# Eight convolution taps of each layer move from VectorE to GpSimd, and two output weight blocks are split by ScalarE

## The chip, the cores and the metric

The kernel runs on one core of a Trainium2 chip. The metric is the device time of one execution in microseconds, as the median of several runs. Weights and inputs start in device memory (HBM), and the result is written there.

## What is computed

Two layers of a hybrid block (layers 0 and 1) over 16 learned meta rows and 512 input rows, and then one second block over the 512 rows. All data are float32. The part that the change touches is the convolution branch of each layer, a causal depthwise convolution of width 31 over 512 channels, and the output projection that adds it to the attention branch:

```python
def conformer_conv_branch(a, g, z, w_dw, b_dw, ln_g, ln_b):
    u = a * jax.nn.sigmoid(g)
    u = lax.conv_general_dilated(u, w_dw[:, None, :], window_strides=(1,),
        padding=[(CONV_WIDTH - 1, 0)], ..., feature_group_count=D_CONV) + b_dw
    u = jax.nn.silu(layer_norm(u, ln_g, ln_b))
    return u * jax.nn.silu(z)
...
    y_attn = dsa_sparse_attention(q, k, v, qi, ki, wi, topk) * jax.nn.silu(za)
    y = jnp.einsum('ble,ed->bld', jnp.concatenate([y_conv, y_attn], axis=-1), w_out[l])
    h = layer_norm(DEEPNORM_ALPHA * h + y, post_ln_g[l], post_ln_b[l])
```

Beside it each layer projects its input to q, k, v, to gates za and zc and to an indexer (qi, ki, wi). The indexer's scores select 132 keys for each query, and the attention runs over these alone.

## The kernel before

**Products in two parts.** TensorE runs in float32r, a shorter float32. To keep the accuracy each operand is split into a high part, the rounded value (`x_hi`, `w_hi`), and a low part, what is left (`x_lo`, `w_lo`), and each product is three passes: hi*hi, hi*lo, lo*hi. The weights stream in as 69 blocks of 128x2048 (`weight_stream`, L106) through a ring of four buffers. SyncE loads a block into `w_raw` once TensorE has done the last product of the block four places earlier (L614). ScalarE copies it rounded into `w_hi` and its negative into `w_lo` (`split_hi`, L693). GpSimd then starts a DMA that adds the block from HBM to the negated copy (`split_lo`, L1158, its DMA is L1162), and TensorE waits for that DMA (L1352). For the blocks in `LO_BY_POOL` (L274) ScalarE makes only `w_hi`, and GpSimd subtracts it from `w_raw` itself in two halves (`subtract_hi`, L1150, L1155). Such a subtraction and such a DMA sit in GpSimd's program at a fixed place. `SPLIT_AT` (L196) says behind which use of a product each block is split: block k2 behind the first product of q, v0 (the first half of v's weights) behind the third, v1 behind the first of k, the first za block behind the third of k.

**Order of a layer.** Each engine has its program in a fixed order. In layer l TensorE runs the products for a and g, the indexer, its scores, then q and k (four channel tiles each, some 6 us a tile), the values of the meta rows (`meta_values`, L1419, which uses v0 and then v1), v, the first gates, and then 40 attention items in layer 0 and 32 in layer 1 (an item is a tile of up to 128 queries and one of 8 heads). Items go in pairs. In each pair TensorE turns the probabilities (L1484, L1490), ScalarE copies them (`probs_t`, L842), TensorE multiplies by v (L1509, L1512) and makes logits for a later pair (L1448), VectorE adds the mask and scales (`masked_logits`, L2021), ScalarE takes the exponentials (L828), and VectorE normalises (L2028, L2030).

**What is woven into the items.** `attention_extras` (L297) hands each engine a list of extra operations for each item. TensorE's fillers are the gates (`GATE_ITEMS`, L226, items 0 to 14) and the output products `wo` (`OUTPUT_AT`, L252: item, half of the columns, row tile, PSUM buffer). The convolution's layer norm runs at items 8 to 20 (`CONV_AT`, L246): turned forward by TensorE (L1533), statistics and two scalings by VectorE (`conv_normed`, L1990, L1997), turned back (L1542), tanh by ScalarE, y by VectorE (L2065, L2069), its high part by ScalarE (L853) and its low part by GpSimd (L1182). `SPLITS_AT` (L278) says at which two items ScalarE splits the halves of a block; GpSimd's part follows in the second of them.

**The taps.** `TAPS` (L283) is the order of the 4 x 31 taps of a layer, four channel tiles c with 31 taps each, all done by VectorE: `conv_acc` becomes u shifted times a weight per channel plus `conv_acc` (`conv`, L1873). Tap 0 is a `tensor_scalar` with the bias (L1884), every other is a `scalar_tensor_tensor` (L1887) that waits for the tap before it of the same channel tile. VectorE does 62 taps before the top-k, then the 17 rounds of the top-k (`topk`, L1923: maxima L1937 and replacements L1946 over score rows of up to 528), 28 taps behind them (up to `TAPS_MASKED`), 7 after the first masked scores (`TAPS_AHEAD`), and 27 in the first eight items (`TAPS_BY_ITEM`). While VectorE is in the top-k, GpSimd waits for a result of its second round (`first_tile_cut`, L1235), and then turns q and k (`rope`, L1186: three `tensor_tensor` of 128x528 for each of 8 channel tiles), with the DMA issues of `next_blocks` between them.

Of the kernel before, what the change touches and what calls it, by code (L numbers as in the profile page):

```python
# [20 lines left out]
ALU = mybir.AluOpType  # L21
# [5 lines left out]
P = 128  # L27
# [3 lines left out]
META = 16  # L31
L = META + SEQ
PAD = 30
TAP_COUNT = PAD + 1
# [205 lines left out]
def gate_needed(l, name, t):  # L240
# [12 lines left out]
    0: ((17, 0, 0, "A"), (19, 0, 1, "B"), (22, 1, 0, "A"), (25, 1, 1, "B"), (27, 0, 2, "A"), (29, 1, 2, "A"),  # L253
        (34, 0, 3, "A"), (36, 1, 3, "A")),
    1: ((17, 0, 1, "A"), (19, 0, 2, "B"), (21, 1, 1, "A"), (23, 1, 2, "A"), (26, 0, 3, "A"), (28, 1, 3, "A")),
# [18 lines left out]
LO_BY_POOL = {NUMBER[key] for key in ((0, "wo", 0, 1), (0, "wo", 1, 1), (1, "a", 0), (1, "g", 0),  # L274
                                      (1, "wo", 0, 1), (1, "wo", 1, 1), (2, "kv", 0), (2, "q", 0))}
# [3 lines left out]
    0: ((0, 1, ("zc", 2)), (2, 3, ("wo", 0, 0)), (5, 6, ("wo", 1, 0)), (12, 13, ("wo", 0, 1)), (17, 19, ("wo", 1, 1))),  # L279
    1: ((0, 1, ("zc", 2)), (2, 3, ("wo", 0, 0)), (7, 8, ("wo", 1, 0)), (12, 13, ("wo", 0, 1)), (17, 17, ("wo", 1, 1))),  # L280
# [5 lines left out]
TAPS += [(1, tap) for tap in range(TAP_COUNT - 11, TAP_COUNT)]  # L286
TAPS += [(2, tap) for tap in range(15)]
for _i in range(TAP_COUNT - 15):
    TAPS += [(2, 15 + _i), (3, _i)]
TAPS += [(3, tap) for tap in range(TAP_COUNT - 15, TAP_COUNT)]  # L290
TAPS_MASKED = 90
TAPS_AHEAD = 97
TAPS_BY_ITEM = (4, 3, 4, 3, 4, 3, 3, 3)
# [92 lines left out]
def build(nc, io, counted):  # L386

    with ExitStack() as ctx:
# [89 lines left out]
        e = [sb(f"exps{i}", [P, L]) for i in range(4)]  # L478
        yt = [sb(f"y_part{i}", [P, CT, P]) for i in range(2)]
        SL_AT = where[0]  # L480
# [93 lines left out]
        tap_done = signal("tap_done")  # L574
        rope_cos = signal("rope_cos")
# [573 lines left out]
        def _(pool):  # L1149
# [47 lines left out]

            def ln_deviation(step, t, rows):
                pool.wait_ge(stats_made.sem, stats_made.at(step))
                reciprocal_deviation(step, meanvar[0:rows, t, 1:2], 1, rows, t, 1.0, LN_EPS)  # L1200
# [17 lines left out]
            for l in range(DEPTH):  # L1218
# [19 lines left out]
                for use in USES[USES.index((l, "q", 0)):USES.index((l, *GATES_AHEAD[l][0]))]:  # L1238
                    if use[1] in ("q", "k"):
                        rope(use)  # L1240
                    next_blocks(use)
                pool.wait_ge(act_took.sem, act_took.at((l, "v", 0)))
# [615 lines left out]
        def _(dve):  # L1858
# [14 lines left out]
            def conv(l, first, last):  # L1873

                x0 = META if l else 0
                for c, tap in TAPS[first:last]:
# [8 lines left out]
                    else:  # L1885
                        dve.wait_ge(tap_done.sem, tap_done.at((l, c, tap - 1)))
# [680 lines left out]
```

## Time and profile before

| | us |
|---|---|
| median of 3 runs | 1025.79 (1024.05 to 1026.18) |
| the profiled execution | 1024.52 |
| its span, first to last instruction | 1022.6 |
| mean granted TensorE clock | 0.993 |

| engine | busy, us | share |
|---|---|---|
| TensorE (PE), matmuls | 987.3 | 97% |
| TensorE, weight loads | 816.8 | 80% |
| VectorE (DVE) | 667.8 | 65% |
| ScalarE (ACT) | 558.8 | 55% |
| GpSimd (POOL) | 231.4 | 23% |

Layer 0 takes roughly the first 350 us, layer 1 the next 310, the second block the rest. In a timeline row stand the start in us from the start of the span, the duration in us, engine, line, operation, output and inputs, and in brackets how long the engine stood idle before and what released it. A busy TensorE is not a TensorE at its peak: the ends of matmuls are modelled. The granted clock is a share of full speed, 2.4 GHz; the other level is 1.2.

### The profile page before, as it was taken

The numbers are of one execution on the slowest core, as the hardware profiler recorded it, in microseconds if no ns is written. First come the engines' busy times: TensorE is split into PE (matmuls) and PEld (weight loads), VectorE is DVE, ScalarE is ACT, GpSimd is POOL, SyncE is SP. The second block draws the span as 40 slices with busy tenths as digits, with TensorE's granted clock in tenths as the row PEclk, the third lists the DMA queues.
The fourth block names the chain that finished last, engine by engine and source line by source line (L and its number), as shares of the span: only waits on it lengthen the run. The fifth ranks groups of instructions, "written<-read, shape, count | busy, mean of one in ns | idle before, by whom it ended". The sixth has DMA issues, their size and how long they took to land.

```text
span 1022.6 us, 15789 instructions
## 1 busy us (share of the span) xinstructions
PE 987.3 (97%) x6084; PEld 816.8 (80%) x6084; DVE 667.8 (65%) x1439; ACT 558.8 (55%) x915; POOL 231.4 (23%) x250
## 2 busy tenths in 40 slices
PE   7999999998999999999999999999999999999997
PEld 7888988886677988888778677888888788888886
DVE  3899999888674489999988756638422333333432
ACT  6685891645333558588165534544646566564442
POOL 0110771115211401077111512634101000000001
PEclk9999999999999999999999899999999999999999
DMA  8876874752001577488464400577777536365662
GB/s 301 196 180 179 210 181 131 166 124 83 1 1 50 157 177 176 124 185 187 124 171 79 156 21 1 171 180 188 176 210 197 114 89 158 90 158 126 175 155 82
DMA packets 23098, 143.92 MB, mean 141 GB/s; under 512 B 2785, under 2 KB 3297, under 8 KB 7281
## 3 DMA queue, kind: packets, MB, share of 16 engines
q0 software_dynamic: 8496, 60.36, 31.7%
q1 hardware_dynamic: 14528, 82.55, 22.8%
q8 instruction: 49, 0.80, 0.3%
q14 instruction: 25, 0.20, 0.1%
HBM read 140.81 MB, written 2.10 MB: 140 GB/s over the span
## 4 chain that ended last, share of the span: by engine, by line
PE 81%; ACT 7%; DVE 5%; DMA 3%; POOL 2%; issue 2%; SPq 0%; POOLq 0%; DVEq 0%; ACTq 0%
PE psum_B L1371 21%; PE psum_A L1371 14%; PE psum_B L1406 7%; PE psum_A L1406 7%; PE psum_A L1568 6%; PE psum_C L1448 3%; PE psum_A L1786 2%; PE psum_B L1568 2%; PE psum_B L1786 2%; PE psum_A L1484 2%; PE psum_B L1512 2%; DVE conv_acc L1887 2%; POOL w_lo L1155 2%; PE psum_B L1773 2%; PE psum_C L1371 1%
## 5 line engine op out<-in xcount | busy, mean ns | idle before, releaser
L1162 POOL DMA_DIRECT2D w_lo<-in_weights x59 | 52.0, 881 | 562.2 <-ACT w_lo L706 536.0
L1887 DVE SCALAR_TENSOR_TENSOR conv_acc<-u,vec,conv_acc 128x528 f32<-128x528 f32 (+1 forms) x240 | 172.3, 755 | 3.2
L1371 PE MATMUL psum_B<-x_hi,w_hi 128*128 128x264 f32 (+3 forms) x472 | 143.9, 338 | 2.5 <-DVE mlp_lo L2341 1.2
L1371 PE MATMUL psum_B<-x_lo,w_hi 128*128 128x264 f32 (+3 forms) x472 | 141.7, 333 | 0.0
L1371 PE MATMUL psum_B<-x_hi,w_lo 128*128 128x264 f32 (+3 forms) x472 | 141.2, 332 | 0.0
L705 ACT ACTIVATE w_hi<-w_raw 128x2048 fp32r<-128x2048 f32 (+2 forms) x73 | 113.4, 1553 | 18.7 <-DMA w_raw<-in_weights 18.2
L1371 PE MATMUL psum_A<-x_hi,w_hi 128*128 128x264 f32 (+3 forms) x408 | 111.1, 311 | 2.0 <-DVE za L2041 0.9
L706 ACT ACTIVATE w_lo<-w_raw 128x2048 fp32r<-128x2048 f32 (+2 forms) x73 | 112.7, 1544 | 0.0
L1371 PE MATMUL psum_A<-x_lo,w_hi 128*128 128x264 f32 (+3 forms) x408 | 109.1, 306 | 0.0
L1371 PE MATMUL psum_A<-x_hi,w_lo 128*128 128x264 f32 (+3 forms) x408 | 109.0, 305 | 0.0
L1371 PEld LDWEIGHTS psum_B<-x_hi,w_hi 128*128 128x128 f32 (+1 forms) x472 | 82.1, 186 | 13.4 <-issue 3.7
L1371 PEld LDWEIGHTS psum_B<-x_hi,w_lo 128*128 128x128 f32 (+1 forms) x472 | 82.0, 187 | 8.9
L1371 PEld LDWEIGHTS psum_B<-x_lo,w_hi 128*128 128x128 f32 (+1 forms) x472 | 82.0, 186 | 8.2
L1371 PEld LDWEIGHTS psum_A<-x_hi,w_hi 128*128 128x128 f32 (+1 forms) x408 | 70.0, 186 | 7.9 <-issue 3.1
L1371 PEld LDWEIGHTS psum_A<-x_hi,w_lo 128*128 128x128 f32 (+1 forms) x408 | 70.0, 186 | 3.4
L1371 PEld LDWEIGHTS psum_A<-x_lo,w_hi 128*128 128x128 f32 (+1 forms) x408 | 70.0, 186 | 3.4
L1946 DVE MATCH_REPLACE8 score<-top,score 128x528 f32<-128x528 f32 (+2 forms) x102 | 56.0, 557 | 0.0
L1937 DVE MAX8 top<-score 128x8 f32<-128x528 f32 (+2 forms) x102 | 51.6, 560 | 1.2 <-POOL score L1231 1.2
L1406 PE MATMUL psum_A<-w_hi,x_hi 128*128 128x512 f32 (+1 forms) x128 | 49.0, 383 | 0.5 <-ACT shifted L764 0.4
L1406 PE MATMUL psum_B<-w_hi,x_hi 128*128 128x512 f32 (+1 forms) x128 | 48.9, 382 | 0.4 <-ACT shifted L764 0.4
L1406 PE MATMUL psum_B<-w_hi,x_lo 128*128 128x512 f32 (+1 forms) x128 | 48.7, 380 | 0.0
L1406 PE MATMUL psum_A<-w_hi,x_lo 128*128 128x512 f32 (+1 forms) x128 | 48.7, 380 | 0.0
(407 smaller groups left out, 2199.5 us busy)
## 6 DMA issues: line engine op xcount, KB each, us to landing
w_raw<-in_weights SPq DMA_DIRECT2D x66, 1024.0 KB, 5.0
w_lo<-in_weights POOLq DMA_DIRECT2D x57, 1024.0 KB, 8.6
h<-in_x SPq DMA_DIRECT2D x1, 2048.0 KB, 11.0
out<-h SPq DMA_DIRECT2D x4, 512.0 KB, 2.6
x_first<-in_x_t SPq DMA_DIRECT2D x3, 528.0 KB, 8.3
post_ln_g<-in_post_ln_g SPq DMA_DIRECT2D x2, 512.0 KB, 4.7
post_ln_b<-in_post_ln_b SPq DMA_DIRECT2D x2, 512.0 KB, 6.1
w_raw<-in_weights SPq DMA_DIRECT2D x2, 288.0 KB, 6.4
```

What stands on the lines that cost most here:

```text
L705: act.activation(whi[n % RING][:, a:b], raw[n % RING][:, a:b], ACT.Copy)
L706: got = act.activation(wlo[n % RING][:, a:b], raw[n % RING][:, a:b], ACT.Copy, scale=-1.0)
L1155: pool.tensor_tensor(wlo[n % RING][:, a:b], raw[n % RING][:, a:b], whi[n % RING][:, a:b].bitcast(F32), ALU.subtract).then_inc(pool_lo.mark ...
L1162: pool.dma_start(wlo[n % RING][:, 0:width], io["weights"][n, :, 0:width], accum_op=ALU.add) \
L1371: mm = pe.matmul(ps[0:cols, i, 0:b - a], w[wp][:, kt, at:at + cols], x[xp][:, kt, a:b], start=(kt == 0 and wp + xp == 0), stop=(kt == KD - ...
L1406: mm = pe.matmul(ps[:, 0, 0:width], act_parts[xp][:, kt, c0:c0 + P], w[wp][:, kk, at:at + width], start=(kt == 0 and wp + xp == 0), stop=( ...
L1448: mm = pe.matmul(banks[odd][0:SIZE[t], i, 0:b - a], qs[s:s + HD, hd // 2, START[t]:END[t]], ks_of[s:s + HD, a:b], start=True, stop=True)
L1568: mm = pe.matmul(ps, x[xp][:, kt, START[t]:START[t] + P], w[wp][:, kk, 0:DC], start=(kt == 0 and wp + xp == 0), stop=(kt == KD - 1 and wp ...
L1786: mm = pe.matmul(ps[:, 0, :], w[wp][:, kt, d % 4 * P:d % 4 * P + P], parts[xp][:, kt, :], start=(kt == 0 and wp + xp == 0), stop=(kt == CT ...
L1887: got = dve.scalar_tensor_tensor(dst, src, w, dst, ALU.mult, ALU.add)
L1937: dve.max(top8[:, t - 1, :], vals).then_inc(topk_max.mark((l, r, t)), 1)
L1946: dve.match_replace(vals, top8[:, t - 1, :], vals, MARK).then_inc(topk_marked.mark((l, r, t)), 1)
```

## The change

Five edits, in both layers:

- GpSimd does taps 0 to 7 of channel tile 3, one behind the rope of each tile of q and k (`tap`, new). VectorE's first tap of that tile is tap 8, and it waits for GpSimd's tap 7. `TAPS` has 116 entries for 124; the places of `TAPS_MASKED` and `TAPS_AHEAD` stay. GpSimd's partial product goes to a new buffer `tap_part`, laid over `y_part`.
- VectorE does 19 taps for 27 in the items.
- `LO_BY_POOL` loses the four blocks (l, wo, 0, 1) and (l, wo, 1, 1): ScalarE makes their negated copies and an accumulating DMA completes them.
- ScalarE splits (l, wo, 0, 1) at items 13 and 15 for 12 and 13, and (1, wo, 1, 1) at 17 and 19 for 17 and 17.
- In layer 0 the first three output products move from items 17, 19 and 22 to 19, 21 and 23, in layer 1 the first from 17 to 18.

```diff
 OUTPUT_AT = {
-    0: ((17, 0, 0, "A"), (19, 0, 1, "B"), (22, 1, 0, "A"), (25, 1, 1, "B"), (27, 0, 2, "A"), (29, 1, 2, "A"),
+    0: ((19, 0, 0, "A"), (21, 0, 1, "B"), (23, 1, 0, "A"), (25, 1, 1, "B"), (27, 0, 2, "A"), (29, 1, 2, "A"),
...
-    1: ((17, 0, 1, "A"), (19, 0, 2, "B"), (21, 1, 1, "A"), ...
+    1: ((18, 0, 1, "A"), (19, 0, 2, "B"), (21, 1, 1, "A"), ...
...
-LO_BY_POOL = {NUMBER[key] for key in ((0, "wo", 0, 1), (0, "wo", 1, 1), (1, "a", 0), (1, "g", 0),
-                                      (1, "wo", 0, 1), (1, "wo", 1, 1), (2, "kv", 0), (2, "q", 0))}
+LO_BY_POOL = {NUMBER[key] for key in ((1, "a", 0), (1, "g", 0), (2, "kv", 0), (2, "q", 0))}
...
-    0: (..., (5, 6, ("wo", 1, 0)), (12, 13, ("wo", 0, 1)), (17, 19, ("wo", 1, 1))),
-    1: (..., (7, 8, ("wo", 1, 0)), (12, 13, ("wo", 0, 1)), (17, 17, ("wo", 1, 1))),
+    0: (..., (5, 6, ("wo", 1, 0)), (13, 15, ("wo", 0, 1)), (17, 19, ("wo", 1, 1))),
+    1: (..., (7, 8, ("wo", 1, 0)), (13, 15, ("wo", 0, 1)), (17, 19, ("wo", 1, 1))),
...
+POOL_TAPS = 8
 TAPS += [(2, tap) for tap in range(15)]
 for _i in range(TAP_COUNT - 15):
-    TAPS += [(2, 15 + _i), (3, _i)]
-TAPS += [(3, tap) for tap in range(TAP_COUNT - 15, TAP_COUNT)]
+    TAPS += [(2, 15 + _i), (3, POOL_TAPS + _i)]
+TAPS += [(3, tap) for tap in range(POOL_TAPS + TAP_COUNT - 15, TAP_COUNT)]
...
-TAPS_BY_ITEM = (4, 3, 4, 3, 4, 3, 3, 3)
+TAPS_BY_ITEM = (3, 3, 3, 2, 2, 2, 2, 2)
...
+            def tap(l, n):
+                x0 = META if l else 0
+                at = V_CONVW + (l * TAP_COUNT + n) * CT + 3
+                w = vec[:, at:at + 1]
+                src = u[:, 3, n + x0:n + L]
+                dst = acc[:, 3, x0:L]
+                if n == 0:
+                    pool.wait_ge(u_made.sem, u_made.at((l, 3)))
+                    b = vec[:, V_CONVB + l * CT + 3:V_CONVB + l * CT + 4]
+                    pool.tensor_scalar(dst, src, w, b, ALU.mult, ALU.add).then_inc(pool_tap.mark((l, 3, n)), 1)
+                    return
+                part = tap_part[:, x0:L]
+                pool.wait_ge(pool_tap.sem, pool_tap.at((l, 3, n - 1)))
+                pool.tensor_scalar(part, src, w, 0.0, ALU.mult, ALU.add).then_inc(pool_step.mark((l, "tap", n)), 1)
+                pool.wait_ge(pool_step.sem, pool_step.at((l, "tap", n)))
+                pool.tensor_tensor(dst, dst, part, ALU.add).then_inc(pool_tap.mark((l, 3, n)), 1)
...
                     if use[1] in ("q", "k"):
                         rope(use)
                     next_blocks(use)
+                    if use[1] in ("q", "k"):
+                        tap(l, use[2] + (0 if use[1] == "q" else CT))
...
-                        dve.wait_ge(tap_done.sem, tap_done.at((l, c, tap - 1)))
+                        if (c, tap) == (3, POOL_TAPS):
+                            dve.wait_ge(pool_tap.sem, pool_tap.at((l, c, tap - 1)))
+                        else:
+                            dve.wait_ge(tap_done.sem, tap_done.at((l, c, tap - 1)))
```

## Rows read from the trace of the kernel before

**Rows 1.** The page's first part: busy time, share of the span, instructions.
```profile
PE 987.3 (97%) x6084; PEld 816.8 (80%) x6084; DVE 667.8 (65%) x1439; ACT 558.8 (55%) x915; POOL 231.4 (23%) x250
```

**Rows 2.** Windows, around items 14 to 18: stretch:length, busy by engine (instructions), granted clock, DMA.
```profile
235.00:240.00 5.00, 3.32 (x29) 2.05 (x26) 4.90 (x9) 1.83 (x8) 1.91 (x2) 1.00 0.62 210
240.00:245.00 5.00, 4.10 (x16) 2.46 (x17) 4.88 (x14) 2.83 (x10) 1.54 (x3) 0.66 0.63 210
575.00:585.00 10.00, 9.01 (x40) 6.04 (x38) 7.69 (x21) 6.84 (x13) 4.38 (x5) 0.66 0.54 190
```

**Rows 3.** Waits of TensorE, whole span: us in total, times, longest.
```profile
PE psum_A L1484 <- ACT probs_t L842: 4.1, 5, 1.5
...
PE psum_C L1542 <- DVE conv_normed L1997: 1.8, 2, 1.5
...
PE psum_B L1371 <- DVE za L2041: 1.1, 2, 0.9
PE psum_B L1542 <- DVE conv_normed L1997: 1.0, 1, 1.0
...
PE psum_A L1371 <- DVE za L2041: 0.9, 1, 0.9
```

**Rows 4.** GpSimd's timeline through q and k, layer 0, and two rows of layer 1.
```profile
103.75 0.29 POOL L1225 TENSOR_SCALAR_AFFINE_SELECT first_tile_negated<-first_tile_negated 128x144 f32<-128x144 f32 x1
110.54 0.20 POOL L1235 TENSOR_SCALAR_AFFINE_SELECT first_tile_cut<-first_tile_cut 128x16 f32<-128x16 f32 x1 [6.49 <-DVE first_tile_cut L1956]
...
124.91 1.33 POOL L1193 TENSOR_TENSOR shifted<-shifted,sin 128x528 f32<-128x528 f32 x1 [0.48 <-ACT shifted L764]
...
129.81 1.33 POOL L1193 TENSOR_TENSOR shifted<-shifted,sin 128x528 f32<-128x528 f32 x1 [0.85 <-ACT shifted L764]
...
133.83 0.87 POOL L1162 DMA_DIRECT2D w_lo<-in_weights  x1
...
460.84 1.33 POOL L1193 TENSOR_TENSOR shifted<-shifted,sin 128x528 f32<-128x528 f32 x1 [0.51 <-ACT shifted L764]
...
464.96 0.89 POOL L1162 DMA_DIRECT2D w_lo<-in_weights  x1
```

**Rows 5.** GpSimd's DMA issues at 133.83, 464.96 and 114.66 us, each alone.
```profile
DMA to landing us min/median/max: 10.3/10.3/10.3
...
DMA to landing us min/median/max: 9.9/9.9/9.9
...
DMA to landing us min/median/max: 8.0/8.0/8.0
```

**Rows 6.** TensorE's timeline: first product of the meta values with v1, both layers.
```profile
145.94 0.39 PE L1413 MATMUL psum_A<-w_hi,meta_hi_lo_in 128*64 128x512 f32 x1
...
476.97 0.39 PE L1413 MATMUL psum_B<-w_hi,meta_hi_lo_in 128*64 128x512 f32 x1
```

**Rows 7.** Groups by line and form, VectorE: taps (busy us, mean ns | idle before).
```profile
L1887 DVE SCALAR_TENSOR_TENSOR conv_acc<-u,vec,conv_acc 128x528 f32<-128x528 f32 x120 | 87.1, 761 | 1.6
```

**Rows 8.** Timelines of GpSimd and VectorE at items 10 to 14 of layer 0.
```profile
226.73 0.75 DVE L1997 SCALAR_TENSOR_TENSOR conv_normed<-conv_normed,rstd,conv_bias 128x512 f32<-128x512 f32 x1
...
231.67 4.78 POOL L1155 TENSOR_TENSOR w_lo<-w_raw,w_hi 128x1024 fp32r<-128x1024 f32 x2
...
234.15 2.85 DVE L1997 SCALAR_TENSOR_TENSOR conv_normed<-conv_normed,rstd,conv_bias 128x512 f32<-128x512 f32 x1
```

**Rows 9.** Timelines of ScalarE, TensorE and VectorE, items 7 and 15 to 18.
```profile
212.03 1.05 ACT L706 ACTIVATE w_lo<-w_raw 128x1024 fp32r<-128x1024 f32 x1
...
238.82 0.63 ACT L853 ACTIVATE x_hi<-y_part 128x512 fp32r<-128x512 f32 x1 [2.86 <-DVE y_part L2069]
...
243.50 0.77 PE L1413 MATMUL psum_A<-w_hi,meta_hi_lo_out 128*64 128x512 f32 x1
...
247.38 0.39 PE L1416 MATMUL psum_A<-w_hi,meta_hi_lo_out 128*64 128x512 f32 x1
...
245.75 0.44 DVE L2021 CUSTOM_DVE_ANT_0 exps<-psum_C,mask 128x272 f32<-128x272 f32 x1
```

## What the change will do to the time

> **What bounds the kernel now.** I read the page first: TensorE is busy for 987.3 us, 97% of the span of 1022.6 [rows 1]. So there are only some 35 us in which it stands still, and no edit to VectorE, ScalarE or GpSimd can return more than that and what the clock takes. The windows of 5 us tell where the clock falls: it is granted 0.66 in 240 to 245 us and 0.66 in 575 to 585 us, and 1.00 just before the first of these [rows 2]. That is 5 x 0.34 = 1.7 us lost in layer 0 and 10 x 0.34 = 3.4 us in layer 1. The first fall comes behind a slice in which TensorE was busy for 3.32 us of 5 [rows 2]. The list of waits names for whom: conv_normed (1.8 + 1.0 us), probs_t copies of ScalarE (4.1 us in 5 waits, one of 1.5), VectorE's za gates (1.1 + 0.9 us) [rows 3]. Last I followed GpSimd in order of time through the projections of q and k, since the change puts its work there [rows 4], and asked when the weight transfers that it issues land [rows 5] and when TensorE first needs them [rows 6].
>
> **Eight taps moved to GpSimd: VectorE's side.** Of 124 taps of a layer VectorE keeps 116. It still does 28 between the last top-k round and the masked scores and 7 behind them; in the turns it does 19 for 27. A tap takes 0.76 us [rows 7], so 8 x 0.76 = 6.1 us leave VectorE in each layer, all from the first eight attention items. These are 6.1 us beside TensorE's gates, not on its path: what they can give back is TensorE's waits for VectorE there, za in rows 3, 2.0 us over both layers, and some of the probs_t waits. I count -2.5 us in all, between 0 and -4.
>
> **GpSimd's side.** A tap there is a tensor_scalar into tap_part and, behind a wait, a tensor_tensor into the accumulator; tap 0 is a tensor_scalar alone. The tensor_tensor has a price: the rope operations of the same 128x528 take 1.33 us [rows 4], with the wait 1.4. The trace of before has no wide tensor_scalar on GpSimd. Its nearest one-input rows are affine_selects, 0.20 us for 128x16 and 0.29 for 128x144 [rows 4]; a line through them gives 0.20 + 4 x 0.09 = 0.56 us at 528. The upper bound is the two-input 1.33, the lower 0.29, the narrow one's own. I take s = 0.65, near the line, since it is nearest in kind. [...]
>
> What matters is what is queued behind the taps. GpSimd issues the accumulating DMA that completes w_lo for each weight block, in program order between the ropes. Block v1 (the second half of v) is issued behind the rope of k0, so behind the ropes of q0 to q3 and, new, taps 0 to 3. Four taps are 4s + 3 x 1.4 = 4s + 4.2 us. GpSimd starts right behind the cut at 110.54 us and until k0's rope stands idle only 0.48 + 0.85 = 1.33 us, waiting for ScalarE [rows 4]. So the issue at 133.83 us slips by 4s + 2.9 = 5.5 us. In layer 1 the one idle row before the issue at 464.96 us is 0.51, so it slips by 4s + 3.7 = 6.3 us [rows 4].
>
> The cover is thin. The issue of 133.83 landed 10.3 us later, at 144.1, and the meta rows' second half, TensorE's first use of v1, starts at 145.94: 1.8 us of slack. In layer 1 it is 464.96 + 9.9 = 474.9 against 476.97: 2.1 us [rows 4 to 6]. So TensorE waits 5.5 - 1.8 = 3.7 us in layer 0 and 6.3 - 2.1 = 4.2 us in layer 1: **+7.9 us**. Bounds: with s = 0.29 and the shortest landing of this stretch, 8.0 us [rows 5], the block lands at 133.83 + 4.1 + 8.0 = 145.9, no wait, and in layer 1 at 464.96 + 4.9 + 8.0 = 477.9, 0.9 us; with s = 1.33 and the landings as they were the waits are 8.2 - 1.8 = 6.4 and 9.0 - 2.1 = 6.9, 13.3 us. I take the landings as they were, since the raw loads they shared the engines with go on. v0, the block before v1, is issued behind only two taps and two ropes earlier, and za's first block is wanted only behind all of v: neither is late.
>
> A gap of some 4 us in TensorE's stream is larger than what stood before either fall of the clock [rows 2]. I count one fall of the smaller size in each layer, 1.7 us: **+3.4 us**, between 0 and 6.8.
>
> All eight taps are 8s + 7 x 1.4 = 15 us of GpSimd, of which its idle gaps take up some; by this estimate it works about 9 us longer than before, into VectorE's 28 taps, which read two SBUF tensors. Rows 8 show what that does: conv_normed at 234.15 took 2.85 us, against 0.75 elsewhere, and ended with GpSimd's w_lo subtraction (231.67 + 4.78). I expect VectorE to lose up to 4 us here, hidden: TensorE is itself about 4 us late by then, and 6.1 us of taps fall away behind it. The Trainium skill (SBUF - State Buffer, on the shared port pair) says the same: a VectorE instruction with two SBUF inputs and a GpSimd instruction that reads SBUF exclude each other for a whole instruction, while one-input maxima do not contend. By that rule the taps beside the maxima are free; by the row alone they need not be.
>
> **Output blocks split by ScalarE.** wo(0,1) and wo(1,1) lose GpSimd's two subtractions (4.78 us) and get ScalarE's negated copies and an accumulating DMA. Gain: the 2.1 us for which VectorE was shut out at 234 [rows 8] (the same in layer 1) go. But ScalarE now does two pieces of 1.05 us at item 15 [rows 9], right ahead of the probs_t copy of item 16. At 238.82 ScalarE had stood idle 2.86 us for that very VectorE result [rows 9]: that comes 2.1 us sooner and the new pieces take 2.1 us. probs_t comes when it did, TensorE waits about 2.5 us in one piece where it waited 1.0 + 1.5, and the clock falls as before: 0, bounds -9.4 (all of conv_normed's 2.8 us, 1.5 us of probs_t and 1.7 + 3.4 us of clock gone) and +2. The new w_lo transfer, 8 to 10 us behind item 15's split, is just in time for its first use.
>
> **Order of the output products.** In layer 0 the meta rows' product moves from item 17 to 19. It was TensorE's filler from 243.50 to 247.6, 4.1 us, while VectorE worked off its conv chain; masked scores 20 and 21 came only at 245.75 [rows 9]. Without it TensorE would be at the logits of item 22 some 2 us before that (my estimate from the rows' order) and must wait for these. I count +2 us (0 to +4.1, the filler's length). In layer 1 the move is 17 to 18, within the same pair of turns: 0, up to +2.5 if its w_lo lands late. The later shifts of layer 0 change the gap between fillers, not their sum.
>
> **Sum.** The profiled execution took 1024.52 us, 1.9 above its span and 1.3 below the median of the three timed ones (1025.79). 1024.5 - 2.5 + 7.9 + 3.4 + 0 + 2 = 1035.3 us. Against the median it would be 1036.6; I forecast **1035.5 us**.
>
> **The rivals.**
> - *Late block, clock stays up.* All as above without 3.4 us: 1032 us. For it: the waits of 0.9 us for za [rows 3] stand in stretches without a fall. Against: rows 2. Chance 0.17.
> - *Faster: the lock and the clock.* If GpSimd's taps are short (s = 0.56) and v1 lands in 8.0 us, the waits are 133.83 + 5.1 + 8.0 - 145.94 = 1.0 and 464.96 + 5.9 + 8.0 - 476.97 = 1.9, 2.9 us. If VectorE, no longer shut out, then keeps TensorE going through items 15 to 17, 9.4 us go, and 2.5 us of gate waits: 1024.5 + 2.9 - 9.4 - 2.5 = 1015.5; with half of the 9.4 it is 1020. It decides as soon as the two waits for v1 stay under some 5 us together and the clock stays at 2.4 GHz at item 16. For it: the fall of the clock is bought by one blocked VectorE instruction in each layer. Against: 1.8 us of slack against 5.5 of slip. Chance 0.25.
> - *Late output weights too.* The w_lo of wo(0,1) and wo(1,1) now need 8 to 10 us from ScalarE's split and come behind TensorE's need in both layers, 2.5 us each, besides the forecast: 1040.5 us. Chance 0.06.
> - *No net effect.* Waits for v1 of 3 to 5 us are paid back by the turns, or GpSimd's taps simply fit in: 1023.5 to 1027.5. Chance 0.07.
> - The forecast: 0.45.
>
> A measurement of this kernel tells about 0.2% (2 us) from no change. Slower: 0.45 + 0.17 + 0.06 = 0.68; same 0.07; faster 0.25. The range goes from the faster rival's middle, 1017, to the dearer taps (s = 1.33, +5.4 us) and late output weights, 1043.
>
> **What would show each step.** GpSimd's tensor_scalar on tap_part at 0.5 to 0.8 us; the DMA issue of v1 near 139.4 and 471.3 us; a TensorE wait before the meta values' second half of some 4 us named as w_lo, with a granted clock under 1.00 behind it; VectorE's taps right behind the top-k longer than 0.76 us; conv_normed at 0.75 us throughout; a TensorE wait for probs_t or VectorE at items 16 to 19. The forecast is wrong if the v1 transfer lands in 8 us, or if the clock no longer falls near 240 and 575 us.

## The result, and the profile after

| | before | after |
|---|---|---|
| median, us | 1025.74 (1024.05 to 1026.18) | 1037.25 (1035.15 to 1038.91) |
| the profiled execution, us | 1024.52 | 1035.83 |
| its span, us | 1022.6 | 1034.0 |
| mean granted clock | 0.993 | 0.985 |

The changed kernel is slower by a factor of 1.0114, with a 95% interval of 1.0088 to 1.0140: +11.7 us. In the changed kernel lines move down: the weight DMA is L1165, probs_t L845, GpSimd's taps L1211 to L1217, `conv_normed` L2023, VectorE's taps L1913.

The page's first part after, to be set beside [rows 1]:

```profile
PE 993.6 (96%) x6084; PEld 821.1 (79%) x6084; DVE 658.9 (64%) x1423; ACT 565.8 (55%) x923; POOL 249.1 (24%) x276
```

VectorE lost 8.9 us of work, less than the 12 that sixteen taps are worth, and TensorE is busy for 6.3 us more with the same 6084 matmuls: they ran at the lower clock. The waits of TensorE after (us in total, times, longest), beside [rows 3]:

```profile
PE psum_A L1507 <- ACT probs_t L845: 8.1, 6, 2.9
...
PE psum_B L1436 <- DMA w_lo<-in_weights: 2.5, 1, 2.5
PE psum_A L1436 <- DMA w_lo<-in_weights: 2.1, 1, 2.1
...
PE psum_B L1535 <- DVE y_part L2083: 1.0, 2, 0.6
...
PE psum_D L1565 <- DVE conv_normed L2023: 0.8, 2, 0.6
...
PE psum_A L1394 <- DVE za L2067: 0.3, 1, 0.3
```

Two waits for v1 are new (4.6 us), probs_t costs 8.1 us for 4.1; conv_normed fell from 2.8 to 0.8 and za from 2.0 to 0.5 (0.3 + 0.2). Windows of 5 us around items 15 to 19 after, beside [rows 2]:

```profile
240.00:245.00 5.00, 2.13 (x9) 1.00 (x9) 3.03 (x11) 4.33 (x11) 2.64 (x4) 0.73 0.99 280
245.00:250.00 5.00, 3.27 (x19) 1.90 (x18) 4.23 (x11) 3.50 (x6) 2.61 (x4) 0.50 0.93 175
250.00:255.00 5.00, 4.60 (x16) 2.65 (x17) 3.63 (x11) 2.83 (x10) 1.00 (x2) 0.50 0.15 31
...
585.00:590.00 5.00, 3.36 (x16) 2.06 (x16) 3.66 (x10) 2.83 (x8) 1.03 (x2) 0.71 0.73 233
590.00:595.00 5.00, 4.90 (x23) 3.54 (x24) 1.89 (x9) 4.66 (x10) 2.50 (x2) 0.50 1.08 262
```

The clock falls at the same two places as before and stays down for longer. Summed over windows of 1 us (each at 0.50 counts 1 us), TensorE was at 1.2 GHz for 3.4 us in layer 0 and 6.8 in layer 1 before; after, for 13.6 (242 to 256 us), 3.4 (532 to 536) and 10.2 (587 to 598). Before rounding that is 27.3 us for 10.2. (The clock falls once more in the last 5 us of the span, when TensorE has no matmul left; that is left out here and below.) Where TensorE had work all the time, half of the difference, 8.5 us, is the cost, and less where it waited anyway.

**GpSimd and v1.** GpSimd's timeline after, around the issue of v1, and the row of that issue's landing:

```profile
133.57 0.71 POOL L1215 TENSOR_SCALAR tap_part<-u,vec 128x528 f32<-128x528 f32 x1
134.36 1.33 POOL L1217 TENSOR_TENSOR conv_acc<-conv_acc,tap_part 128x528 f32<-128x528 f32 x1
...
139.62 0.90 POOL L1165 DMA_DIRECT2D w_lo<-in_weights  x1
140.29 1.00 POOL L1215 TENSOR_SCALAR tap_part<-u,vec 128x528 f32<-128x528 f32 x1
```
```profile
DMA to landing us min/median/max: 8.8/8.8/8.8
```

TensorE then, at the meta values' second half:

```profile
148.46 0.45 PE L1436 MATMUL psum_A<-w_hi,meta_hi_lo_in 128*64 128x512 f32 x1 [2.09 <-DMA w_lo<-in_weights]
```

**ScalarE at items 15 to 18.** ScalarE's timeline after, with TensorE's two waits below it:

```profile
239.00 0.63 ACT L856 ACTIVATE x_hi<-y_part 128x512 fp32r<-128x512 f32 x1 [1.23 <-DVE y_part L2095]
...
240.60 1.04 ACT L708 ACTIVATE w_hi<-w_raw 128x1024 fp32r<-128x1024 f32 x1
241.54 1.04 ACT L709 ACTIVATE w_lo<-w_raw 128x1024 fp32r<-128x1024 f32 x1
242.49 0.42 ACT L845 ACTIVATE probs_t<-psum_A 128x320 f32<-128x320 f32 x1
...
248.03 1.05 ACT L708 ACTIVATE w_hi<-w_raw 128x1024 fp32r<-128x1024 f32 x1
248.97 1.04 ACT L709 ACTIVATE w_lo<-w_raw 128x1024 fp32r<-128x1024 f32 x1
249.92 0.42 ACT L845 ACTIVATE probs_t<-psum_A 128x320 f32<-128x320 f32 x1
```
```profile
242.96 0.69 PE L1507 MATMUL psum_A<-ident,exps 128*128 128x128 f32 x2 [2.87 <-ACT probs_t L845]
...
250.40 0.69 PE L1507 MATMUL psum_A<-ident,exps 128*128 128x128 f32 x2 [1.55 <-ACT probs_t L845]
```

Two pairs of pieces stand right ahead of a probs_t, one for (wo, 0, 1) and one for (wo, 1, 1), and between them TensorE has no output product any more.

### The profile page after: what moved, and what is told of

It is laid out like the page before. It is cut to its first block, busy times and chain, and to the rows that moved or that the text cites. A ratio compares the mean times of both kernels' runs of the same rounds, so it can differ in the third digit from the quotient of the medians.

```text
span 1034.0 us, 15807 instructions
## 1 busy us (share of the span) xinstructions
PE 993.6 (96%) x6084; PEld 821.1 (79%) x6084; DVE 658.9 (64%) x1423; ACT 565.8 (55%) x923; POOL 249.1 (24%) x276
## 4 chain that ended last, share of the span: by engine, by line
PE 67%; DVE 12%; issue 7%; ACT 7%; POOL 5%; DMA 1%; SPq 0%; POOLq 0%; DVEq 0%; ACTq 0%
PE psum_B L1394 16%; PE psum_A L1394 8%; PE psum_B L1429 7%; PE psum_A L1429 6%; PE psum_A L1591 6%; DVE score L1972 3%; DVE conv_acc L1913 3%; DVE top L1963 3%; PE psum_A L1809 2%; PE psum_B L1535 2%; PE psum_B L1591 2%; PE psum_B L1809 2%; PE psum_A L1507 2%; POOL w_lo L1158 2%; PE psum_B L1796 1%
## 5 line engine op out<-in xcount | busy, mean ns | idle before, releaser
L1165 POOL DMA_DIRECT2D w_lo<-in_weights x63 | 55.8, 885 | 554.5 <-ACT w_lo L709 528.4
L1913 DVE SCALAR_TENSOR_TENSOR conv_acc<-u,vec,conv_acc 128x528 f32<-128x528 f32 (+1 forms) x226 | 165.7, 774 | 2.8
L708 ACT ACTIVATE w_hi<-w_raw 128x2048 fp32r<-128x2048 f32 (+2 forms) x81 | 121.7, 1503 | 17.4 <-DMA w_raw<-in_weights 17.0
L709 ACT ACTIVATE w_lo<-w_raw 128x2048 fp32r<-128x2048 f32 (+2 forms) x81 | 121.1, 1495 | 0.0
L2054 DVE RECIPROCAL prob_rsums<-prob_sums 128x1 f32<-128x1 f32 (+1 forms) x72 | 11.5, 160 | 63.6 <-ACT exps L831 63.4
L845 ACT ACTIVATE probs_t<-psum_A 128x192 f32<-128x192 f32 (+2 forms) x48 | 20.8, 433 | 52.6 <-PE psum_A L1513 52.3
## 6 DMA issues: line engine op xcount, KB each, us to landing
h<-in_x SPq DMA_DIRECT2D x1, 2048.0 KB, 10.2
```

Source lines behind the costliest of these rows:

```text
L708: act.activation(whi[n % RING][:, a:b], raw[n % RING][:, a:b], ACT.Copy)
L709: got = act.activation(wlo[n % RING][:, a:b], raw[n % RING][:, a:b], ACT.Copy, scale=-1.0)
L845: act.activation(dst[:, 0:t * P + REST], bank["A"][:, 0, 0:t * P + REST], ACT.Copy) \
L1165: pool.dma_start(wlo[n % RING][:, 0:width], io["weights"][n, :, 0:width], accum_op=ALU.add) \
L1913: got = dve.scalar_tensor_tensor(dst, src, w, dst, ALU.mult, ALU.add)
```

## The experiments

Theory A, after this first look: the taps cost only the two waits for v1 (some 3 us net); the rest is the output blocks, through pieces ahead of probs_t and the clock behind them. Theory B: the taps carry it. Theory C, which came up behind the first runs: the output product that moved away from item 17 was TensorE's filler there, and without it VectorE's chain is late, whichever engine splits the blocks. The runs; us are (ratio - 1) x 1025; the last column is TensorE's time at 1.2 GHz in the profiled execution (before 10.2, after 27.3):

| run | what | ratio to before (95%) | us | at 1.2 GHz |
|---|---|---|---|---|
| e1 | taps alone | 1.0031 (1.0020-1.0043) | +3.2 | 17.1 |
| e2 | blocks and order alone | 1.0073 (1.0060-1.0086) | +7.5 | 20.5 |
| e3 | after, taps behind k | 1.0121 (1.0108-1.0134) | +12.4 | 20.5 |
| e4 | after, pieces one item earlier | 1.0116 (1.0102-1.0129) | +11.9 | 23.9 |
| e5 | after, pieces in ScalarE's idle time | 1.0082 (1.0069-1.0095) | +8.4 | 20.5 |
| e6 | order alone | 1.0048 (1.0035-1.0061) | +4.9 | 13.7 |
| e7 | after, taps behind k, 22 taps for 28 | 1.0065 (1.0046-1.0084) | +6.7 | 20.5 |
| e8 | taps alone, behind k, 22 for 28 | 0.9973 (0.9962-0.9984) | -2.8 | 6.8 |
| e9 | blocks alone, old order | 1.0125 (1.0108-1.0141) | +12.8 | 13.6 |
| e10 | e8, subtraction in quarters | 0.9989 (0.9979-0.9999) | -1.1 | 6.8 |
| e11 | e7 and e5, products at 18, 20, 22 | 1.0031 (1.0020-1.0043) | +3.2 | 13.6 |
| e12 | e8, (wo, 1, 1) by ScalarE | 0.9997 (0.9988-1.0006) | -0.3 | 10.3 |

The last column holds for one execution each, and not always for a typical one. In e1 and e2 the profiled execution was the slowest of six (1031.5 us where the others took 1027.0 to 1029.1, and 1035.5 where they took 1031.1 to 1032.4); in e6 and e9 its mean granted clock, 0.993 and 0.992, was above that of every other execution of the run (0.988 to 0.992, and 0.987 to 0.990). A difference of 3.4 us between two rows of that column, one short fall, says nothing by itself.

### e1 and e2: the two halves of the change

e1 takes `OUTPUT_AT`, `LO_BY_POOL` and `SPLITS_AT` of the kernel before into the changed one; e2 takes those three of the changed kernel into the one before.

> The kernel before with the taps alone: eight taps of channel tile 3 on GpSimd, 19 for 27 taps of VectorE in the items; output blocks, split places and output products as before. Theory A (the loss of the changed kernel lies in ScalarE's split pieces ahead of probs_t and in the clock that falls behind them; GpSimd's taps cost only the two waits for v1): the waits for w_lo before the meta values stay at 2.1 + 2.5 = 4.6 us, the clock is low for about 10 us as before, VectorE's waits for za (2.0 us) shrink by 1.5: 1024.5 + 4.6 - 1.5 = 1027.6 us, ratio 1.003. Theory B (the taps on GpSimd are what costs, through the late block and a clock that falls for longer behind it): 1032 us or more, ratio 1.007 or more.

> The kernel before with the output blocks alone: LO_BY_POOL, SPLITS_AT and OUTPUT_AT of the changed kernel, all taps on VectorE. Theory A: no wait for v1; the probs_t waits of 2.9, 1.6 and 2.2 us near items 16 to 18 are there, the low clock lasts 20 us or more for 10: 1024.5 + 7 = 1031 to 1033 us, ratio 1.007. Theory B: within 2 us of the kernel before, 1023 to 1026 us.

Theory A gave 1027.6 and 1031 to 1033 us; the medians are 1028.2 and 1031.9. 3.2 + 7.5 = 10.7 of the 11.7 us. B is out. The profiled execution of e1 took 1031.5, above its median: behind the v1 wait of layer 1 (2.4 us, ended at 483.9) its clock did fall, and again behind a wait for VectorE at 190:

```profile
190.00:195.00 5.00, 4.36 (x25) 4.17 (x26) 4.52 (x18) 3.01 (x9) 0.00 (x0) 0.66 0.90 159
485.00:490.00 5.00, 5.00 (x17) 3.52 (x15) 5.00 (x16) 3.25 (x4) 4.92 (x5) 0.67 0.09 34
```

So the fall that I predicted there can come, but after has none at the same waits. The profiled execution of e2 took 3.6 us more than its median at the same mean clock (0.989) as four of the other five; in it TensorE waits 3.0 us for the w_lo of an output block in layer 1 (at 594). Whether the faster executions lack that wait no trace shows.

### e3 and e7: what stands behind the wait for v1

```diff
-                    if use[1] in ("q", "k"):
-                        tap(l, use[2] + (0 if use[1] == "q" else CT))
+                    if use[1] == "k":
+                        tap(l, 2 * use[2])
+                        tap(l, 2 * use[2] + 1)
```

> The changed kernel with GpSimd's eight taps all placed behind the weight issues of the tiles of k, two behind each, so that no tap stands ahead of the issue of v1. Theory A: v1 is issued near 134 us, no wait for w_lo before the meta values (4.6 us gone), the rest as in the changed kernel: 1035.8 - 4.6 = 1031.2 us; ratio to the kernel before 1.0065. Theory B: most of the loss goes, 1027 us or less. A rival inside A: the taps of k now end later on GpSimd, VectorE's ninth tap of channel tile 3 waits, and less than 2 us are saved.

v1 is issued at 134.00 and no wait for it is left, as expected, and yet nothing was saved (1.0121 for 1.0114). VectorE of the kernel before behind the top-k, then VectorE and TensorE of e3:

```profile
157.35 0.22 DVE L1970 TENSOR_SCALAR mask<-first_tile_negated 128x144 bf16<-128x144 f32 x1
157.50 1.01 DVE L1974 TENSOR_SCALAR mask<-score 128x272 bf16<-128x272 f32 x3
```

```profile
157.33 0.80 DVE L1997 TENSOR_SCALAR mask<-first_tile_negated 128x144 bf16<-128x144 f32 x1
158.05 2.05 DVE L2001 TENSOR_SCALAR mask<-score 128x272 bf16<-128x272 f32 x3
160.02 0.86 DVE L1908 TENSOR_SCALAR conv_acc<-u,vec 128x528 f32<-128x528 f32 x1
160.91 23.54 DVE L1914 SCALAR_TENSOR_TENSOR conv_acc<-u,vec,conv_acc 128x528 f32<-128x528 f32 x27
184.37 0.15 DVE L2048 CUSTOM_DVE_ANT_0 exps<-psum_C,mask 16x16 f32<-16x16 f32 x1
```
```profile
184.79 0.17 PE L1472 MATMUL psum_C<-k,q 64*16 64x16 f32 x1 [0.74 <-DVE neg_max L2048]
190.54 0.17 PE L1514 MATMUL psum_A<-ident,exps 16*16 16x16 f32 x1 [2.29 <-DVE exps L2057]
...
524.25 0.36 PE L1472 MATMUL psum_C<-k,q 64*128 64x144 f32 x1 [2.11 <-DVE neg_max L2048]
```

Before, the two mask rows took 0.22 and 1.01 us, and the first masked scores came 21.5 us after the mask began (157.35 to 178.89); after needs 26.0 (157.42 to 183.41), e3 27.0. GpSimd's last ropes and taps run beside these instructions, until 162.3 us in after and 165 in e3. In e3 the masked scores of layer 0 come 5.5 us later than before and TensorE waits 0.7 + 2.3 = 3.0 us for them, so by my estimate it had some 2.4 us of slack there. In after the 4.5 us of layer 0 are hidden by that slack and by TensorE's own 2.1 us behind v1 (0.5 us is left, a wait for exps at 189.6). Without the wait for v1 VectorE is what is late, over both layers 0.7 + 2.3 + 2.1 = 5.1 us for 4.6.

The third expectation named a wait for GpSimd's last tap; there is none, VectorE is slowed before it comes to tap 8.

```diff
-TAPS_MASKED = 90
-TAPS_AHEAD = 97
-TAPS_BY_ITEM = (3, 3, 3, 2, 2, 2, 2, 2)
+TAPS_MASKED = 84
+TAPS_AHEAD = 91
+TAPS_BY_ITEM = (4, 3, 3, 3, 3, 3, 3, 3)
```

> The changed kernel with GpSimd's taps behind k (as in the earlier run, where no wait for v1 was left but VectorE came 3 us late to the first masked scores: waits of 0.7 + 2.3 us in layer 0 and 2.1 in layer 1), and with 22 taps of VectorE between the top-k and the masked scores for 28, 25 in the items for 19. Theory A: neither the 4.6 us for v1 nor the 5.1 us for VectorE is left: 1036.5 - 5 = 1031.5 us. A rival: the six taps that move into the items come back as waits for za and zc there (about 2 us), 1033.5.

Measured 1030.9 (by the ratios 5.0 us below after): the waits for v1 and those for VectorE behind the top-k are both gone. Four of its six executions took 1029.9 to 1031.1 us and two 1035.1 and 1035.9; the traced one is of the four. Fewer taps with GpSimd's where the change put them was not run. For za TensorE waits 1.0 + 0.2 us in layer 0, as before the change [rows 3]; the rival's 2 us did not come.

### e8: the taps alone, placed so

> The kernel before with the taps alone (output blocks, split places and output products as before), GpSimd's taps behind k, 22 taps between the top-k and the masked scores, 25 in the items. Theory A: no wait for v1, none for VectorE behind the top-k, the falls of the clock as before: 1024.7 - 0.5 = 1024.2 us, the same as the kernel before; the 3.5 us that the taps alone cost are the v1 waits, less what VectorE gives back. A rival: GpSimd's taps lock VectorE's for 3 us a layer and this shows wherever the taps stand: 1027 us.

Measured 1022.9 us, better than I expected and faster than the kernel before: 0.9973 (0.9962 to 0.9984). No wait for v1 and none for VectorE behind the top-k; in layer 1 the waits for za and for a masked score (0.9 + 0.3 us before) are gone, and the fall of the clock there lasts 3.4 us for 6.8:

```profile
240.00:245.00 5.00, 3.40 (x14) 2.03 (x15) 4.85 (x15) 2.75 (x11) 1.93 (x3) 0.68 0.68 210
575.00:580.00 5.00, 3.70 (x15) 2.11 (x14) 4.86 (x14) 3.01 (x8) 2.01 (x3) 0.66 0.87 312
```

The profiled execution is 1.7 us shorter than that of before, the medians differ by 2.8. Of waits 1.2 us are gone, but 0.6 us came back elsewhere (conv_normed at 243.1, 0.3; probs_t at 576.3, 0.25), and half of the 3.4 us at the low clock is 1.7: the clock is the larger part. It is so in the untraced executions too, the mean granted clock is 0.995 or 0.996 in five of six of e8 and at most 0.995, mostly 0.994, in the twelve of before beside them. So sixteen taps are worth some 3 us when they delay neither v1 nor the masked scores, and cost 3.2 us where the change put them.

### e6 and e9: order and blocks apart

> The kernel before with the output products' order alone (layer 0: 19, 21, 23 for 17, 19, 22; layer 1: 18 for 17). The prediction gave +2 us. Theory A (ScalarE's pieces carry the loss, the order little): 1024.7 + 2 = 1026.7 us. Theory C (the missing filler carries it): 1029 us or more, with a wait of 2 us or more for masked logits, probs_t or exps at items 17 to 19 of layer 0 and a low clock of 13 us there.

The order alone costs 4.9 us where the prediction had 2. TensorE in e6, where the product at item 17 had been [rows 9]:

```profile
243.26 0.63 PE L1542 MATMUL psum_D<-ident,conv_normed 128*128 128x128 f32 x4 [0.74 <-DVE conv_normed L1997]
...
245.56 0.44 PE L1512 MATMUL psum_B<-probs_t,v 128*64 128x128 f32 x4 [1.30 <-DVE y_part L2057]
...
247.90 0.69 PE L1484 MATMUL psum_A<-ident,exps 128*128 128x128 f32 x2 [1.27 <-ACT probs_t L842]
```

3.3 us in three waits, in place of the filler, and the low clock of layer 0 lasts 6.8 us for 3.4. (In layer 1, where the product moves by one item, a wait of 0.8 us for y_part is new.) The extra fall runs into the product itself when it comes: its matmuls take 0.63 us for 0.39 from 250.78 on.

e9 has the blocks of the changed kernel, the products of the one before:

> The kernel before with LO_BY_POOL and SPLITS_AT of the changed kernel, but the output products where they were (17, 19, 22; 17). It asks whether the products had to move. Blocks and order together cost 7.2 us, the order alone 4.9. If ScalarE's pieces cost by themselves only what is left (2.3 us), this run gives 1024.7 + 2.3 = 1027 us. But the w_lo of (wo, 0, 1) is issued at about 243 us and lands 8 to 10 us later, at 251 to 253, and the meta rows' product at item 17 wants it at about 247: a wait for w_lo of 4 to 6 us in layer 0 and 2 to 5 in layer 1 in place of the missing filler, 1031 to 1036 us.

Measured 1038.0: 5.3 us more than e2, which has the same blocks and the new order, and the intervals lie apart. (From the whole change, 1.0114, it can't be told.) TensorE and the landing of the w_lo that was issued at 241.40:

```profile
250.09 0.41 PE L1412 MATMUL psum_A<-w_hi,meta_hi_lo_out 128*64 128x512 f32 x1 [3.62 <-POOL x_lo L1181]
```
```profile
DMA to landing us min/median/max: 8.6/8.6/8.6
```

241.4 + 8.6 = 250.0: the row names GpSimd's x_lo, the last by the profile, which was done at 249.1; it was the DMA. In layer 1 the product waits 4.1 us more for its w_lo. So the order had to move with the blocks, and the two are one edit of 7.5 us. They do not simply add: the new order costs 4.9 us while GpSimd splits the blocks (e6) and saves 5.3 once ScalarE does (e2 beside e9).

### e4, e5, e11: where ScalarE's pieces stand

```diff
-(13, 15, ("wo", 0, 1)), (17, 19, ("wo", 1, 1))
+(13, 14, ("wo", 0, 1)), (16, 18, ("wo", 1, 1))
```

> The changed kernel with ScalarE's split pieces one item earlier: (wo, 0, 1) at items 13 and 14 for 13 and 15, (wo, 1, 1) at 16 and 18 for 17 and 19, in both layers, so that a piece stands where ScalarE is idle for 1.2 and 2.2 us behind the probs_t of the odd item and not right ahead of the next pair's. Theory A: the probs_t waits of 2.9 and 1.6 us in layer 0 fall to about 2 and 0, the 2.2 of layer 1 to about 1.5, and the low clock from 27 us to 14 or less: 1035.8 - 3 - 6 = 1027 to 1031 us. A rival (VectorE's chain without the output product as a filler is what is late, whatever ScalarE does): 1034 to 1036 us.

The time did not change and neither did the two waits (2.87 and 1.55 us again), and this was my mistake in reading the program: the items of a pair run in one list between two probs_t copies, so a piece at item 14 still stands behind the y copy that ScalarE waits for and ahead of probs_t of item 16. e5 puts it at the head of the list:

```diff
+            todo["act"][i].insert(0, ("split", NUMBER[(l, *key)], 0))
+            todo["act"][j].insert(0, ("split", NUMBER[(l, *key)], 1))
```

(for (wo, 1, 1); for (wo, 0, 1) the second only)

> The changed kernel with the second piece of (wo, 0, 1) right behind the probs_t copy of item 15 and the first and second piece of (wo, 1, 1) right behind those of items 17 and 19, each ahead of the y copies of its item, where ScalarE stood idle for 1.2 and 2.2 us. The run with pieces one item earlier left them behind the y copies and so ahead of the next pair's probs_t: its waits of 2.87 and 1.55 us did not move. Theory A (a piece ahead of probs_t is what TensorE waits for): 2.87 falls to about 2.0 and 1.55 to 0, in layer 1 2.16 to about 1.2; the low clock falls from 27 us to 17 or less; 1036 - 3.4 - 4 = about 1029 us. Theory C (VectorE's chain masked logits to exponentials to normalised is what is late without the output product as filler, so a wait of the same length stays under VectorE's name): 1034 us or more.

Measured 1034.1: at C's bound of 1034, and 3.5 us below e4, the intervals apart, so the place of the pieces ahead of probs_t does cost something. The probs_t waits did fall, 2.87 to 1.53 and 1.55 to 0, but conv_normed took their place. ScalarE, GpSimd, VectorE and TensorE of e5:

```profile
239.72 0.62 ACT L862 ACTIVATE x_hi<-y_part 128x512 fp32r<-128x512 f32 x1
```
```profile
240.18 0.92 POOL L1171 DMA_DIRECT2D w_lo<-in_weights  x1 [6.51 <-ACT w_lo L715]
240.85 1.55 POOL L1191 TENSOR_TENSOR x_lo<-y_part,x_hi 128x512 fp32r<-128x512 f32 x1
...
242.76 0.56 POOL L1183 TENSOR_TENSOR rstd<-var_eps,minus_half 128x1 f32<-128x1 f32 x1
```
```profile
243.36 0.75 DVE L2029 SCALAR_TENSOR_TENSOR conv_normed<-conv_normed,rstd,conv_bias 128x512 f32<-128x512 f32 x1 [0.52 <-POOL rstd L1183]
```
```profile
244.25 1.00 PE L1571 MATMUL psum_D<-ident,conv_normed 128*128 128x128 f32 x4 [1.37 <-DVE conv_normed L2029]
```

The piece pushed the y copy back by some 0.5 us (239.72 for 239.00, of which e5 was 0.2 late before); GpSimd's x_lo comes behind that, its rstd behind x_lo in program order, VectorE's second scaling behind rstd, TensorE behind that.

The edit moved one thing more. GpSimd issues the block's DMA in the item of the second piece, so the issue went from item 15 to 14 with it. In e5 it stands at 240.18, ahead of x_lo; in after it stood behind x_lo and rstd:

```profile
239.71 1.27 POOL L1185 TENSOR_TENSOR x_lo<-y_part,x_hi 128x512 fp32r<-128x512 f32 x1 [6.20 <-ACT x_hi L856]
...
242.94 0.92 POOL L1165 DMA_DIRECT2D w_lo<-in_weights  x1 [1.06 <-ACT w_lo L709]
```

x_lo of e5 starts 1.1 us behind the start of the y copy (0.7 in after) and takes 1.55 us (1.27 in after), and VectorE stands idle 0.52 us for rstd. So about 0.5 of the 1.37 us is the issue's, not the missing filler's, by my estimate from these rows. e4 and e11 have it too (in e4 the wait for conv_normed at 245.9 is 1.90 us). No run has the pieces in idle time and the issue where it was. Without a filler the chain of four engines is what TensorE waits for, whichever piece of it is late. e11 takes e7, e5 and the first product one item sooner (18, 20, 22 for 19, 21, 23):

> All that the runs so far point to: the changed kernel with GpSimd's taps behind k, 22 taps ahead of the masked scores, ScalarE's pieces in its idle time (item 14 and items 16, 18, ahead of the y copies), and the output products of layer 0 at items 18, 20, 22 for 19, 21, 23. Theory A (pieces and taps out of the way, filler nearly where it was): 1034.1 (idle pieces) - 5.6 (taps) - 2 (filler one item sooner) = 1026.5 us. Theory C (without a product at item 17 VectorE's chain is late there, whoever splits the blocks): the waits of 1.4, 0.7 and 0.9 us for conv_normed and y_part of the run with idle pieces stay, and 1028 to 1029 us.

1028.6: theory C's 1028 to 1029. The waits of e5 are still there (1.5, 1.4, 0.6 us). TensorE stops for 0.9 us more inside the product, at 250.7, just when the w_lo of (wo, 0, 1) has landed (238.7 + 11.9 us), and for 1.4 us in layer 1 for a w_lo of wo. Beside e8, which has the same taps, the blocks cost 6 us even so.

### e10 and e12: is there a free way for one block?

e10 cuts GpSimd's subtraction of (wo, 0, 1) from 2 x 128x1024 to 4 x 128x512:

> The kernel of the last run (GpSimd's taps behind k, 22 taps ahead of the masked scores, output blocks as in the kernel before; 1022.9 us) with GpSimd's subtraction for (wo, 0, 1) in four pieces of 128x512 for two of 128x1024, in both layers. If conv_normed of VectorE at 234 us takes 2.85 us because it waits for the end of one GpSimd instruction of 2.4 us, it takes 1.8 us or less now; TensorE's waits of 1.03 and 1.5 us for it fall to about 0 and 0.5, the low clock from 7 us to 4 or less: 1022.9 - 2.5 = 1020.4 us. If VectorE is shut out for as long as GpSimd has such work at all, or if GpSimd's four pieces take longer than its two, nothing changes: 1022.5 to 1024 us.

VectorE of e10, beside 2.85 us in [rows 8]:

```profile
233.34 0.77 DVE L2062 TENSOR_SCALAR exps<-exps,prob_rsums 128x272 f32<-128x272 f32 x1
234.03 1.76 DVE L2029 SCALAR_TENSOR_TENSOR conv_normed<-conv_normed,rstd,conv_bias 128x512 f32<-128x512 f32 x1
...
235.90 1.19 DVE L2062 TENSOR_SCALAR exps<-exps,prob_rsums 128x272 f32<-128x272 f32 x1
```

conv_normed comes 1 us sooner, as expected, but the next pieces then shut VectorE out of the `normalise` behind it (1.19 us, elsewhere 0.36), GpSimd needs 5.5 us for 4.8, and y comes when it came: TensorE's wait of 1.03 us for conv_normed fell away (0.17 for a conv_tanh stand in its place), the one for probs_t rose from 1.54 to 2.12 and the next one for conv_normed from 0.31 to 0.74. No gain; against e8 the ratio is 0.9989 to 0.9973, the intervals overlap. Seven of its twelve executions took 1022.6 to 1023.7 us at a mean clock of 0.993 to 0.995, and five 1026.1 to 1027.0 at 0.991 to 0.993; the traced one is of the seven.

e12 moves only (wo, 1, 1), into ScalarE's idle time, with the product kept at item 17:

> The kernel of the run with taps behind k and 22 taps ahead of the masked scores (1022.9 us), with one of the two output blocks of a layer alone moved from GpSimd to ScalarE: (wo, 1, 1), its pieces right behind the probs_t copies of items 17 and 19, ahead of the y copies; (wo, 0, 1) stays with GpSimd and the products where they were. If a split by ScalarE is free where ScalarE is idle and the product at item 17 is kept, the time stays: 1021.5 to 1023.5 us, with no probs_t wait at item 18. Then what costs in the changed kernel is the first block, whose split comes too late for the product at item 17, and not the second. If ScalarE's pieces cost wherever they stand (y copies and tanh later, hence conv_normed and y_part), 1025 us or more; if the w_lo of (wo, 1, 1) lands too late for its product in layer 1, a wait of 1 to 3 us for it and 1025 us.

1024.7 us, 2.5 above e8 by the ratios and the interval lies above e8's. The pieces at 242.4 and 250.3 us stand in idle time, TensorE's waits around them are those of e8 (0.3 less at one place), none is for the w_lo of a wo block. What its profile shows more than e8's is a wait of 0.8 us for another block's w_lo at 695 us, in the second block, and 6.8 us at the low clock in layer 1 for 3.4, half of which is 1.7. Whether the pieces cause either is open; the clock fell behind the same waits in both. It does not carry most of the 2.5 us: five of the eleven executions had a mean clock of 0.996 or 0.997, at or above e8's, and their median is still 1024.5. And e8 was measured once, beside other executions of before: the interval of e12 overlaps that of e10, which has the same taps.

## Why the prediction held in its sum and failed in its parts

The forecast was 1035.5 us, the time is 1037.25. The sum came out by luck, because two errors cancelled: the taps were priced at -2.5 + 7.9 + 3.4 = +8.8 us and cost 3.2 (e1), the blocks and the order at 0 + 2 = +2 and cost 7.5 (e2).

- **The price of a tap, and the slip: right.** tensor_scalar took 0.69 to 0.73 us (taken: 0.65), and 0.96 to 1.07 just behind a DMA issue; the last tap of each layer, which runs beside VectorE's masks, took 1.1. v1 was issued at 139.62 us (forecast 139.4), in layer 1 at 478.07, where all is 6.85 us later by then: a slip of 6.3, as forecast.
- **The landing: the mis-sized term.** I kept 10.3 and 9.9 us; it took 8.8 and 8.4. The waits were 2.1 and 2.5 us for 3.7 and 4.2. I had argued that the raw loads shared the engines with it and go on; issued 6 us later it landed sooner. It does so throughout: in the four traces with taps ahead of the issue (after, e1, e4, e5) v1 landed in 7.9 to 8.8 us, in the ten others, where the issue is early, in 9.4 to 10.3. Why is not shown.
- **A fall of the clock in each layer behind that wait: did not come** in after, came once in the profile of e1. TensorE had stood for 2 us, not 4.
- **VectorE's gift in the turns: too large.** za waits fell by 1.5 us in after, but 0.7 of that only because the wait for v1 had come first: e7 and e8, where TensorE is on time, have the 1.0 us of layer 0 again. What stays is 0.9 + 0.3 us in layer 1. The probs_t waits of the first items (0.42, 0.71 and 0.41 us) are the same in both kernels.
- **VectorE shut out behind the top-k, "up to 4 us, hidden": right**, 4.5 us in layer 0, and e3 shows what it hid behind: 2.1 us of TensorE's wait for v1, for the 4 that I gave it, and 2.4 us of slack that I had not counted. The sentence mattered more than its zero in the sum told: it makes the v1 wait worth nothing to remove alone. The top-k beside GpSimd's taps ended when it had (157.4 us; maxima 566 ns for 560), while the one-input mask rows took twice as long. By the Trainium skill (SBUF — State Buffer, Who interferes with whom) a VectorE instruction with two SBUF inputs contends with a GpSimd instruction that reads SBUF, one in a two-port mode (which tensor_scalar can enter) contends with GpSimd, and any other does not. The trace agrees on the taps (two inputs) and on the maxima; that the mask rows ran in a two-port mode it does not show, only that they took twice as long. My prediction had drawn on the first and the last and not on the two-port modes.
- **The output blocks at 0: the step that failed.** Beside the order alone they cost 2.6 us more (7.5 less 4.9), and with the old order 12.8 (e9). The first half of the step came as written: conv_normed took 0.75 us at 236.42, y came sooner against TensorE, the two pieces ate it, and TensorE waited 2.87 us in one piece for "about 2.5". What I left out is the second pair of pieces, (wo, 1, 1) at item 17, ahead of probs_t of item 18: 1.55 us, in the stretch from which the same change takes the filler. I had "the clock falls as before"; it was low for 13.6 us for 3.4 there, and 10.2 for 6.8 in layer 1. e5 bears the pieces out: out of the way of probs_t they cost 3.5 us less than in e4.
- **The order at +2: mis-sized**, 4.9 (e6). The waits (3.3 us) were near the estimate, the longer fall of the clock behind them was not in it. The two edits were priced one by one, each against the trace of before.
- **Late output weights** (a rival at 0.06) did not show in the profiled execution of after, but did in layer 1 of e2 (3.0 us), e3 (1.3), e5 (1.0) and e11 (1.4) and in both layers of e9 (3.6 and 4.1). It is the reason for the order. In after the executions lie at 1035.2, 1035.8, 1038.7 and 1038.9 us and their mean clocks do not sort them (0.987, 0.985, 0.985, 0.987), so what makes 3 us between them is open.

The rival "faster" was wrong at its root: it held that an unblocked VectorE would keep TensorE going through items 15 to 17. With the pieces in idle time and VectorE unblocked (e5, e11) TensorE still waits there, though both lack the product at item 17; with it in place the w_lo is late (e9).

The upper end of the range was added up wrongly: 1035.5 with 5.4 us for dearer taps and 5 for late output weights is 1045.9, not 1043.

## What to carry to other kernels

Price a filler that moves by the fall of the clock that it had been preventing, not by its length alone, and price edits to one stretch together. When a wait is removed, ask which engine it was covering: here 4.5 us of VectorE in layer 0 lay behind 2.1 us of TensorE's wait and 2.4 of its slack. Taking away the wait alone gave nothing back (e3), with fewer taps ahead of the masked scores it gave 5 us (e7) and made the taps a gain (e8). Work that is moved to another engine should stand behind those of its DMA issues that are awaited, an issue that is moved should not come to stand ahead of awaited work (e5), and the same number of instructions should leave the stretch whose end is awaited, not one that has slack.

## What the runs showed of the hardware

- A one-input f32 tensor_scalar of 128x528 on GpSimd takes 0.71 us, a two-input one 1.33. Right behind a DMA issue of its own either is some 0.3 us longer (0.98 to 1.07 for the one-input form; for x_lo, two inputs of 128x512, 1.55 in e5 for 1.27 in after). Beside VectorE's masks and taps GpSimd is slowed as well: 1.08 us for a one-input tap at 159.5 in e3, 1.66 for a two-input one at 163.3, with no issue before them.
- VectorE beside GpSimd: maxima and replacements are not slowed (a replacement of 128x528 takes 0.69 us at 108.5, with GpSimd idle, and at 111.8, beside it, in before), two-input taps, bf16 masks from f32 scores (1.01 to 2.05 us for three) and f32 tensor_scalars (0.36 to 1.19) are. Cutting GpSimd's work into smaller instructions spreads the time in which VectorE is shut out and does not shorten it (e10).
- The same w_lo transfer of 1 MB, v1, landed 7.9 to 8.8 us after its issue where that came 6 us late (four traces), and 9.4 to 10.3 us after it where it came early (ten). What decides this is not shown.
- The clock: behind waits of the same length TensorE was at 1.2 GHz in one execution and not in another (2.4 and 2.5 us for v1 in layer 1, in e1 with a fall and in after without; 0.42 + 0.71 us at item 4 of layer 1, with one of 3.4 us in after and none before). A single profile does not price it.
